# Attention row buffers as a ring of sixteen 512-column pieces, with row statistics kept for four steps

## What is computed

```python
o_a = _diff_attention(qa, ka, va, rel_bias, lam)        # p0 - lam * p1, two softmaxes per head
o_a = _rmsnorm(o_a, diff_head_norm[l]) * (1.0 - lam_init)
o_b = _stick_breaking(sb_q, sb_k, sb_v)                 # sigmoid(z) * product of sigmoid(-z) to its right
o_c = _forgetting_attention(f_q, f_k, f_v, log_f)       # softmax with a decay
o_m = _memory_attention(m_q, km, vm)                    # softmax over 256 memory keys
y = concat(o_a, o_b, o_c, o_m) * silu(gate)
x = x + _rmsnorm(y @ w_out[l], post_norm[l])
```

## Time and profile before

| | before |
|---|---|
| median of three runs | 2931.33 us |
| the profiled execution, its own time | 2925.86 us |
| its span (first to last instruction) | 2924.0 us |
| PE busy | 2737.3 us, 94% of the span |
| DVE busy | 2154.1 us, 74% |
| ACT busy | 1616.5 us, 55% |
| mean granted TensorE clock | 0.973 |

### The profile page before, as it was taken

One profiled execution on the slowest core, in us unless ns is written; L12 is line 12 of the kernel. 1 busy time (PEld: TensorE's weight loads), 2 busy tenths in 40 slices (PEclk: granted clock), 3 DMA queues, 4 the chain that ended last, 5 costly groups with the idle time before them and its releaser, 6 DMA issues. The chain is left out here.

```text
span 2924.0 us, 76171 instructions
## 1 busy us (share of the span) xinstructions
PE 2737.3 (94%) x29978; PEld 1970.3 (67%) x29978; DVE 2154.1 (74%) x5964; ACT 1616.5 (55%) x4307; POOL 194.4 (7%) x854
## 2 busy tenths in 40 slices
PE   2679999999999999999999999999999999779998
PEld 2357777778777777787777777877777778534443
DVE  6555898888768988888689988786898888631111
ACT  4324665557756655677566556675665566631212
POOL 0000001310000013100000131000001310000000
PEclk6789999999999999999999999999999999989999
DMA  3232102020111120211111202102112010153331
GB/s 105 69 92 59 44 20 71 16 58 24 43 43 40 29 71 16 54 27 33 53 38 31 71 16 51 29 28 58 38 30 69 10 38 24 48 183 102 107 110 43
DMA packets 178810, 152.82 MB, mean 52 GB/s; under 512 B 10988, under 2 KB 169588, under 8 KB 178444
## 3 DMA queue, kind: packets, MB, share of 16 engines
q1 hardware_dynamic: 178008, 146.90, 18.3%
q0 software_dynamic: 448, 1.05, 0.1%
HBM read 79.66 MB, written 26.84 MB: 36 GB/s over the span
## 5 line engine op out<-in xcount | busy, mean ns | idle before, releaser
L1074 PE MATMUL job<-wt,big 128*128 128x128 f16 x10752 | 684.3, 219 | 15.3 <-DVE gate_s L1354 13.7
L1074 PE MATMUL job<-big,wt 128*128 128x512 f16 x2688 | 667.6, 380 | 6.0 <-PEq L621 4.1
L1074 PEld LDWEIGHTS job<-wt,big 128*128 128x128 f16 x10752 | 632.1, 98 | 59.6 <-DVE gate_s L1354 21.5
L1448 DVE TENSOR_TENSOR turned_halves<-turned,turned_halves 128x512 f16<-128x512 f32 (+3 forms) x864 | 490.1, 588 | 93.6 <-ACT turned_halves L1227 90.9
L1227 ACT CAST turned_halves<-turned 128x512 f16<-128x512 f32 (+3 forms) x864 | 426.2, 520 | 217.0 <-PE turned L1134 212.5
L1240 ACT ACTIVATE rows<-rows,neg_max 128x512 f32<-128x512 f32 (+3 forms) x704 | 449.2, 642 | 87.4 <-DVE neg_max L1320 85.9
L1134 PE MATMUL turned<-ident,rows 128*128 128x128 f32 x2848 | 437.6, 276 | 11.1 <-DVE turned_halves L1448 6.5
L1120 PE MATMUL scores<-stack 128*128 128x512 f16 (+3 forms) x1600 | 425.5, 347 | 8.6 <-DMA stack<-planes 6.2
L1149 PE MATMUL mixed<-values,turned_halves 128*128 128x64 f16 (+1 forms) x8544 | 411.5, 199 | 5.2 <-issue 2.3
L1149 PEld LDWEIGHTS mixed<-values,turned_halves 128*128 128x128 f16 x8544 | 373.9, 98 | 59.1 <-DVE turned_halves L1448 17.8
L1074 PEld LDWEIGHTS job<-big,wt 128*128 128x128 f16 x2688 | 250.7, 98 | 237.1 <-issue 7.5
(11 more groups left out here) (147 smaller groups left out, 2666.1 us busy)
## 6 DMA issues: line engine op xcount, KB each, us to landing
stack<-planes SPq DMA_DIRECT2D x160, 192.0 KB
ws<-w_in SPq DMA_DIRECT2D x56, 512.0 KB, 4.0
y_halves<-y_out_halves SPq DMA_DIRECT2D x64, 256.0 KB, 2.5
rows<-y_halves SPq DMA_DIRECT2D x16, 1024.0 KB, 7.9
rows<-x SPq DMA_DIRECT2D x16, 512.0 KB, 3.6
ws<-w_out SPq DMA_DIRECT2D x16, 512.0 KB, 3.9
stack<-x SPq DMA_DIRECT2D x16, 512.0 KB, 4.7
out<-stack SPq DMA_DIRECT2D x16, 512.0 KB, 2.9
```

Of the source, the lines that this page charges most:

```text
L1074: last = nc.tensor.matmul(dst, lhs, rhs, start=(k0 == 0 and q == 0), stop=(k1 == KT and q == len(pairs) - 1))
L1448: nc.vector.tensor_tensor(turned[:, tau % PT_RING, 1, 0:w], t_bank[tau % T_BANKS][:, 0:w], turned[:, tau % PT_RING, 0, 0:w], ALU.subtract) \
```

## The change

`rows_flat` keeps its size, 32 KB per partition, but is used as 16 pieces of 512 columns: chunk n lies in piece n % 16 (`scored`). A piece is free when the turn of chunk n - 16 is done, or, for row 1 of a diff step, its combine (`freed_by`). The planner no longer asks the scores for the turns of step g - 2; in its place each softmax copy and each second sigmoid of a stick chunk asks for the piece it writes, and at run time `row_free` waits for it, on DVE for the 704 softmax chunks and on ACT for the 320 stick chunks. `ROWS` is 8, so the statistics of four steps are kept, and a row's maximum waits for `post` of step g - 4. All ranks and the other numbers of the planner are new, so the order of operations on each engine changes throughout the block. The other buffers (`temps` with five slots, three score banks, two turn banks, the ring of four halves, the two places of `gate_s` and `y_f`) stay as they are. So do the first and the last block.

```diff
-    "pe": {"turn": 0.51, "gate": 4.65, "y": 5.37, "mix": 5.92, "score": 6.18, "project": 6.81},
-    "act": {"hi": 1.61, "take": 2.14, "job": 3.54, "stick": 4.05, "exp": 4.14, "convert": 8.98},
-    "dve": {"low": 0.24, "lo": 0.37, "post": 1.31, "weigh": 1.70, "combine": 2.21, "near": 3.30,
-            "widen": 3.71, "copy": 4.28, "scan": 8.79},
+    "pe": {"gate": 0.42431, "turn": 2.20151, "mix": 5.35782, "y": 5.37000, "score": 5.80587, "project": 6.80653},
+    "act": {"take": 1.61000, "job": 1.87479, "hi": 3.54000, "exp": 4.13816, "stick": 6.82325, "convert": 8.98000},
+    "dve": {"low": -0.84756, "lo": 0.89170, "post": 1.31000, "widen": 3.71000, "copy": 4.28000,
+            "weigh": 4.92499, "combine": 6.68901, "near": 6.69658, "scan": 8.78954},
...
-AHEAD = {0: 0.93, 1: 0.52, 2: 0.14, 3: 0.14}
-SLACK, LATE = 1.04, 4.77
-S_BANKS, T_BANKS, J_BANKS, PT_RING, ROWS = 3, 2, 2, 4, 4
+AHEAD = {0: 0.91866, 1: 0.63275, 2: 0.13067, 3: 0.20070}
+SLACK, LATE = 1.07577, 6.67812
+S_BANKS, T_BANKS, J_BANKS, PT_RING, ROW_RING, ROWS = 3, 2, 2, 4, 16, 8
...
+        self.freed_by = {}
+        for g in range(self.n_steps):
+            for tau, m, k0, _ in self.t_chunks[g]:
+                self.freed_by[self.chunk_at(g, m, k0)] = ("turn", tau)
+                if self.kinds[g] == "diff":
+                    self.freed_by[self.chunk_at(g, 1, k0)] = ("combine", tau)
...
-                if g >= 2:
-                    need.append(("turn", self.t_chunks[g - 2][-1][0]))
...
+                    if n >= ROW_RING:
+                        need.append(self.freed_by[n - ROW_RING])
...
-                    q["copy"].append((("copy", n), ("copy", g, ch), [("score", n)], 0.2 + w * 0.00104, 0.0))
+                    q["copy"].append((("copy", n), ("copy", g, ch),
+                                      [("score", n)] + ([self.freed_by[n - ROW_RING]] if n >= ROW_RING else []),
+                                      0.2 + w * 0.00104, 0.0))
...
-                                      + ([("post", g - 2)] if g >= 2 else []), 0.17, 0.0))
+                                      + ([("post", g - ROWS // 2)] if g >= ROWS // 2 else []), 0.17, 0.0))
...
-        def row(g, m):
-            return rows[:, (2 * g + m) % ROWS, :]
+        def scored(n, c0, c1):
+            at = n % ROW_RING * BANK
+            return rows_flat[:, at + c0:at + c1]
+
+        def row_free(eng, n):
+            if n >= ROW_RING:
+                what, tau = plan.freed_by[n - ROW_RING]
+                if what == "turn":
+                    eng.wait_ge(t_full, tau + 1)
+                else:
+                    eng.wait_ge(combined, DIFF_TAU[tau] + 1)
...
+                    row_free(act, n)
+                    nc.scalar.activation(scored(n, 0, w), s_bank[n % S_BANKS][:, 0:w], ACT.Sigmoid) \
...
                     dve.wait_ge(s_full, n + 1)
-                    nc.vector.tensor_scalar(row(g, m)[:, c:c + w], s_bank[n % S_BANKS][:, 0:w], 1.0,
+                    row_free(dve, n)
+                    nc.vector.tensor_scalar(scored(n, 0, w), s_bank[n % S_BANKS][:, 0:w], 1.0,
```

More of the change, by code:

```diff
@@ L51 @@
 RANK = {
-    "pe": {"turn": 0.51, "gate": 4.65, "y": 5.37, "mix": 5.92, "score": 6.18, "project": 6.81},
-    "act": {"hi": 1.61, "take": 2.14, "job": 3.54, "stick": 4.05, "exp": 4.14, "convert": 8.98},
-    "dve": {"low": 0.24, "lo": 0.37, "post": 1.31, "weigh": 1.70, "combine": 2.21, "near": 3.30,
-            "widen": 3.71, "copy": 4.28, "scan": 8.79},
-    "pool": {"root": 0.00},
-    "sp": {"stacks": 0.00, "pairs": 0.50, "strip": 1.00, "sums": 2.00, "store": 3.00, "near_in": 4.00},
-}
-AHEAD = {0: 0.93, 1: 0.52, 2: 0.14, 3: 0.14}
-SLACK, LATE = 1.04, 4.77
-S_BANKS, T_BANKS, J_BANKS, PT_RING, ROWS = 3, 2, 2, 4, 4
+    "pe": {"gate": 0.42431, "turn": 2.20151, "mix": 5.35782, "y": 5.37000, "score": 5.80587, "project": 6.80653},
+    "act": {"take": 1.61000, "job": 1.87479, "hi": 3.54000, "exp": 4.13816, "stick": 6.82325, "convert": 8.98000},
+    "dve": {"low": -0.84756, "lo": 0.89170, "post": 1.31000, "widen": 3.71000, "copy": 4.28000,
+            "weigh": 4.92499, "combine": 6.68901, "near": 6.69658, "scan": 8.78954},
+    "pool": {"root": 0.00000},
+    "sp": {"stacks": 0.00000, "pairs": 0.50000, "strip": 1.00000, "sums": 2.00000, "store": 3.00000,
+            "near_in": 4.00000},
+}
+AHEAD = {0: 0.91866, 1: 0.63275, 2: 0.13067, 3: 0.20070}
+SLACK, LATE = 1.07577, 6.67812
+S_BANKS, T_BANKS, J_BANKS, PT_RING, ROW_RING, ROWS = 3, 2, 2, 4, 16, 8
 Q, K, V, G = range(4)
@@ L139, in __init__ @@
                     tau += 1
+        self.freed_by = {}
[4 more added lines that the diff above has]
+                    self.freed_by[self.chunk_at(g, 1, k0)] = ("combine", tau)
+        n = max(self.freed_by) + 1
         self.stick_n = [n for g in range(self.n_steps) if self.kinds[g] == "stick" for n, *_ in self.chunks[g]]
@@ L512, in build @@
         values = [sb(f"values{b}", [P, NT, 2, P], F16) for b in range(2)]
-        rows_flat = sb("rows", [P, ROWS * max(SEQ, 2048)], F32)
-        rows = rows_flat[:, 0:ROWS * max(SEQ, 2048)].rearrange("p (r s) -> p r s", r=ROWS)
+        rows_flat = sb("rows", [P, ROW_RING * BANK], F32)
+        rows = rows_flat[:, 0:4 * max(SEQ, 2048)].rearrange("p (r s) -> p r s", r=4)
         ws = sb("ws", [P, 2, KT * P], F32)
@@ L1134, in turn @@
                         last = nc.tensor.transpose(t_bank[tau % T_BANKS][:, k * P:(k + 1) * P],
-                                                   row(g, m)[:, (k0 + k) * P:(k0 + k + 1) * P], ident[:, :])
+                                                   scored(plan.chunk_at(g, m, k0), k * P, (k + 1) * P), ident[:, :])
                     last.then_inc(t_full, 1)
@@ L1202, in stick_parts @@
                         .then_inc(stick_u, 1)
-                    nc.scalar.activation(row(g, m)[:, c:c + w], s_bank[n % S_BANKS][:, 0:w], ACT.Sigmoid) \
+                    row_free(act, n)
+                    nc.scalar.activation(scored(n, 0, w), s_bank[n % S_BANKS][:, 0:w], ACT.Sigmoid) \
                         .then_inc(stick_beta, 1)
@@ L1236, in _ @@
                         n, m, c, w = args[1]
-                        mine = row(g, m)[:, c:c + w]
+                        mine = scored(n, 0, w)
                         act.wait_ge(max_ready, ROW_OF[g, m] + 1)
@@ L1301, in weigh @@
                     keys = w - 1 if last else w
-                    mine = row(g, m)[:, c:c + keys]
+                    mine = scored(n, 0, keys)
                     after = plan.slots[n][0] * BANK + 1
@@ L1343, in combine @@
                         dve.wait_ge(coef_step, at + 4)
-                    s = slice(k0 * P, (k0 + tiles) * P)
-                    nc.vector.scalar_tensor_tensor(row(g, 0)[:, s], row(g, 1)[:, s], sc[:, 1:2],
-                                                   row(g, 0)[:, s], op0=ALU.mult, op1=ALU.add) \
+                    first, second = (scored(plan.chunk_at(g, b, k0), 0, tiles * P) for b in range(2))
+                    nc.vector.scalar_tensor_tensor(first, second, sc[:, 1:2], first, op0=ALU.mult, op1=ALU.add) \
                         .then_inc(combined, 1)
```

## The result

The changed kernel takes 2949.78 us (median, 2945.26 to 2950.6) against 2930.95 us for the kernel before on the same chip: a ratio of 1.0061, with a 95% interval of 1.0043 to 1.0078. It is slower by 19 us, where 15 us less was forecast, and lies above the stated range. The profiled execution took 2949.14 us, its span is 2947.0 us, 23.0 us more than before. Among the runs further down, one execution of e3 and one of e10 had the granted clock at about two thirds throughout (4099.17 and 4094.95 us), and their times and traces are left out.

The account below looks back on a forecast made before the run. PE, busy 94% of the span, was taken as the bound, with only its pauses to change. Terms -8 - 4 - 3 - 3 + 3 = -15 us took 2931.33 to 2916.3 us; range 2890 to 2944 us.

Parts of the forecast that it names:

- Unit changes: PE's waits for DMAs into `stack` at unit starts: larger chunk stock covers them, gain 4 us, bounds 0 and 8.4.
- the added waits: 704 DVE copies and 320 ACT sigmoids get one more wait each: cost 3 us.
- The waits for unfinished rows: PE weight loads waiting on rows, 30.3 us: fall under 20; gain 8 us, bounds 2.3 and 30.3.
- `gate_s` was to stay near 15: Sign in the after profile: PE's waits for `gate_s` to free a job bank stay near 15 us.
- The term for row statistics: Mem units, statistics kept for four steps: gain 3 us, bounds 0 and 6.8.
- The new ranks: New ranks and look-ahead numbers, throughout the block: taken as nothing, bounds plus and minus 10 us.
- The end of the block: Drain after the last score, 6.4 us idle: earlier last scores gain 3 us.
- DVE's and ACT's busy times: Sign in the after profile: both stay within 1%, as no instruction changes size.
- the sum: All terms on the whole kernel: -15 us, giving a predicted time of 2916.3 us.
- the much faster rival: Stick, diff and mem units pack nearly without gaps like forget units: about -45 us, 2886 us; chance 0.13.
- The slower rival: DVE held by copies whose piece is not yet turned: +18 us on PE, 2949 us; chance 0.17.

Follow-up runs that it names:

- e3: Kernel before (whole rows) with the new RANK, AHEAD, SLACK and LATE; 2980.11 us.
- e10: Kernel before, lists untouched, with four extra transfers ahead of each stick, diff and forget unit's first stack transfers; 2968.5 us, ratio 1.0134.
- e1: Changed kernel with the planner's landing time for stack transfers 6.0 us (forget 6.6, mem 3.6) instead of 3.6; 2915.26 us, ratio 0.9953.
- e3b: Repeat of e3: kernel before with the new RANK, AHEAD, SLACK and LATE, whole rows kept; 2980.69 us, ratio 1.018.
- e2: Changed kernel with RANK, AHEAD, SLACK and LATE of the kernel before; 2963.91 us, ratio 1.0117.
- e11: Changed kernel, lists untouched, with a unit's stack transfers counted on two semaphores, one per half of the heads; 2954.57 us, ratio 1.0088.
- e10b: Repeat of e10: kernel before, lists untouched, four extra transfers ahead of units' first stack transfers; 2964.08 us, ratio 1.0133.
- e5: Kernel before, order unchanged, with one more wait ahead of each softmax copy and each second sigmoid; 2924.5 us, ratio 0.9985.

## Why the prediction was wrong

**The step that failed is "Unit changes".** It said that a larger stock of unturned chunks covers the 8.4 us of waits, gave the bounds 0 and 8.4, and took a gain of 4. In the changed kernel the waits grew by 16.3 us, with 10.2 us of clock behind them. A stock covers nothing by being there: the fixed list must place its turns between the last scores of one unit and the first of the next. The list placed 4.4 us there, as its number for the transfers asked. The prediction took only the waits of before as its bound, and no loss was allowed for, though the kernel before had the means: its trace has transfers issued 0.6 us apart, four or seven of them, and its code the planner's 3.6 us. In the kernel before the same wrong number did little harm, because from diff to forget, for one, the list happened to hold enough that the first scores came 9 us after the last, with no wait.

**The clock was left out.** The prediction read 1.00 in all units but the first and counted PE's pauses at their length only. In the changed kernel six of the eight waits of 2.0 to 2.6 us cost 1.7 us more behind them.

**The other terms.** None of them was priced by a run of its own, but for the added waits. The waits for unfinished rows (30.3 us of weight loads) were to fall below 20: they are 11.4 + 8.7 + 3.6 = 23.7 in the changed kernel and 21.8 in e1, less of a fall than said, but in the right place. That the ring makes it is seen with the new ranks (67.7 us in e3b); with the old ones it brings 0.4 us (e2), so the 8 us of this term hold only together with ranks that suit. `gate_s` was to stay near 15: it is 14.0 us, 9.0 of it now at line 1189's transpose of y. Before, with the 1.8 us at that transpose, it was 17.5, so it fell by 3.5 and did not go; it was right not to count it away. The term for row statistics put all 15.7 us of it into the mem units; the trace of before has 12.6 there, which makes its bound 9.9 us and not 6.8. The added waits cost nothing where they are always satisfied (3 us were taken). The new ranks were priced at nothing, within 10 us either way; with whole rows they cost 52 us (e3b), with the ring they are 14 us faster than the old ones (2949.8 against 2963.9 in e2). Ranks and layout can't be priced apart, and that bound was too narrow. The end of the block was to give 3 us and gave none: 6.5 us idle of 16 in the drain, after 6.4 of 17. DVE's and ACT's busy times moved by 0.4%. Freed of the stall, the kernel takes 2915.3 us, where the sum said 2916.3. That agreement is partly luck: e1 has other lists than the changed kernel, and its unit changes gave 5.8 us, not 4. The price of the much faster rival also adds up to 49.7 us (29.7 + 10 + 10), not 45, which changes none of the conclusions.

**The slower rival had the time and the wrong mechanism.** It said 2949 us by copies that hold DVE. They held it 5.0 us, 9 times, where 22 times and 24 us were named as the least that decides. The time was hit by chance; a mechanism is proven only by its own line in the trace. The fact that the looser need would let the scores of a unit finish early was in the prediction, as a benefit only.

## What to carry to other kernels

When a fixed order is made by a cost model, loosening a constraint hands more of the decision to the model's numbers, so check first those that the old constraint kept harmless, above all transfer times: count the issues on the queue, not just one landing. At each point where one buffer is emptied and filled again, compare the time from the last reader to the first new reader with the work that the order has between them. A stall of two or more microseconds on a TensorE that is otherwise full cost about its whole length here, and often some time at half clock behind it.

## What the hardware showed

- The granted clock fell to half after six of the changed kernel's eight waits of 2.0 to 2.6 us (before the first scores of a stick or forget unit), for 3.4 us each time; before each it had been at 1.00 for 78 us or more. After the changed kernel's waits of 0.7 to 0.9 us before the diff units it did not fall. In e11 it also fell five times where the wait had been cut in two, with no part over 1.8 us. In e10b it did not fall after waits of 2.3 to 3.7 us before the four diff units, so the length of the wait alone does not decide.
- 1024 more waits that were always satisfied cost no time (e5, ratio 0.9985, 0.9976 to 0.9994).
- Transfers of 192 KB and less, awaited together, were mostly issued 0.6 to 0.9 us apart on the SP queue. In the changed kernel the first scores behind seven of them started 6.4 to 6.6 us after the first issue, and behind four of them after 5.5 to 6.5 us.
